# The chunk inverse of a delta-rule mixer: the masked factor as one 128x128 block with zero quadrants

## The reference, cut to what matters

```python
def wkv7_scan(s0, r, w, k, v, a, b):
    def step(s, inp):
        r_t, w_t, k_t, v_t, a_t, b_t = inp
        sa = jnp.einsum('bhij,bhj->bhi', s, a_t)
        s = s * w_t[:, :, None, :] + sa[..., :, None] * b_t[..., None, :] + v_t[..., :, None] * k_t[..., None, :]
        y = jnp.einsum('bhij,bhj->bhi', s, r_t)
        return s, y
    ...
    s_last, ys = lax.scan(step, s0, xs)
```

## Time and profile before

| | |
|---|---|
| median of 3 runs | 1065.11 us (1059.28 to 1065.58) |
| the profiled execution | 1064.27 us |
| its span, first to last instruction | 1062.5 us |
| granted TensorE clock, mean | 0.984 of full speed |
| busy in the span: PE / PEld / DVE / ACT / POOL | 985.0 / 728.9 / 552.9 / 374.0 / 461.4 us |

### The profile page before, as it was taken

How to read it: one execution, slowest core, us unless ns; L and a number is a source line. 1 busy time by engine, 2 the same in 40 slices (tenths; PEclk the granted TensorE clock), 3 DMA queues, 4 the chain that set the end, 5 groups by cost and what they waited for, 6 DMA issues and landing times. The chain is left out here.

```text
span 1062.5 us, 22807 instructions
## 1 busy us (share of the span) xinstructions
PE 985.0 (93%) x9433; PEld 728.9 (69%) x9433; DVE 552.9 (52%) x1176; ACT 374.0 (35%) x764; POOL 461.4 (43%) x505
## 2 busy tenths in 40 slices
PE   5999999979989989999999999999998999997885
PEld 4777787768878778888787888884554555554442
DVE  6587776757666527777455465333374222221125
ACT  3444446546666524444344440100121111111013
POOL 7647565257868457877732344410001222221110
PEclk9999999989999999999999999999998999999997
DMA  8022221030000056420351224408888999999985
GB/s 270 0 85 80 85 85 40 0 87 5 4 4 5 4 139 183 141 64 2 106 159 42 78 79 159 159 0 312 365 323 339 414 415 415 415 416 415 411 342 236
DMA packets 86000, 182.86 MB, mean 172 GB/s; under 512 B 9897, under 2 KB 59589, under 8 KB 78218
## 3 DMA queue, kind: packets, MB, share of 16 engines
q1 hardware_dynamic: 79325, 168.59, 43.7%
q0 software_dynamic: 5088, 8.43, 2.1%
q10 hardware_dynamic: 1485, 4.39, 1.1%
HBM read 172.98 MB, written 17.55 MB: 179 GB/s over the span
## 5 line engine op out<-in xcount | busy, mean ns | idle before, releaser
L2429 POOL DMA_INDIRECT d_y<-tl_xn,ex_sidx x32 | 32.1, 1002 | 113.2 <-DVE tl_xn L3021 105.6
L2424 POOL DMA_INDIRECT tl_xn<-d_tok,ex_gidx x16 | 16.9, 1053 | 139.4 <-DVEq L3012 76.5
L3017 DVE SCALAR_TENSOR_TENSOR ex_sg<-tl_psA,ex_slot_rs,ex_sg 128x128 f32<-128x128 f32 x32 | 11.2, 351 | 124.6 <-ACT ex_sg L2788 124.5
L264 PE MATMUL psv<-xT,w_sum 128*128 128x260 f32 x256 | 61.7, 384 | 1.2 <-DVE uv_gu L1702 0.6
L226 POOL TENSOR_TENSOR w_sum<-w 128x512 f32<-128x512 f32 x16 | 21.2, 1327 | 94.2 <-PE mg_w L264 94.0
L2788 ACT ACTIVATE ex_sg<-tl_psA,ex_slot_rs 128x128 f32<-128x128 f32 x32 | 11.8, 368 | 123.4 <-PE tl_psA L2622 122.1
L264 PEld LDWEIGHTS psv<-xT,w_sum 128*128 128x128 f32 x256 | 48.3, 190 | 9.9 <-issue 1.3
L264 PE MATMUL rk_ps<-xT,rk_w 128*128 128x260 f32 x208 | 50.1, 384 | 0.0
L264 PE MATMUL rk_ps<-xS,rk_w 128*128 128x260 f32 x200 | 48.6, 386 | 0.0
L264 PEld LDWEIGHTS rk_ps<-xT,rk_w 128*128 128x128 f32 x208 | 39.3, 190 | 6.7 <-issue 0.8
L264 PEld LDWEIGHTS rk_ps<-xS,rk_w 128*128 128x128 f32 x200 | 37.4, 190 | 8.0 <-issue 2.5
(11 more groups left out here) (637 smaller groups left out, 2713.6 us busy)
## 6 DMA issues: line engine op xcount, KB each, us to landing
wd<-in_moe_w_down SPq DMA_DIRECT2D x13, 1024.0 KB, 22.9
rk_w<-in_w_in SPq DMA_DIRECT2D x12, 1024.0 KB, 5.4
w_uv<-in_w_in SPq DMA_DIRECT2D x16, 512.0 KB, 5.3
w<-in_w_in SPq DMA_DIRECT2D x8, 1024.0 KB, 5.9
tl_x<-in_moe_w_down SPq DMA_DIRECT2D x8, 1024.0 KB, 19.0
xT<-in_moe_w_gate SPq DMA_DIRECT2D x5, 1024.0 KB
xT<-in_moe_w_up SPq DMA_DIRECT2D x5, 1024.0 KB
w<-in_proj_a SPq DMA_DIRECT2D x4, 1024.0 KB, 5.7
```

The source lines that it names most:

```text
L264: ins = eng.matmul(bank[:, 0:TH], w[:, k, :], x[:, k, :], start=(first and k == 0), stop=(last and k == NK // 2 - 1), skip_group_check=True)
L2424: eng.indirect_dma_start(out=xg[:, p % 2, :], out_offset=None, in_=m.d_tok, in_offset=bass.IndirectOffsetOnAxis(ap=gidx[:, p:p + 1], axis= ...
L2429: eng.indirect_dma_start(out=m.d_y2, out_offset=bass.IndirectOffsetOnAxis(ap=rows, axis=0), in_=yo[:, x, :], in_offset=None, bounds_check= ...
L3017: eng.scalar_tensor_tensor(out=sg[:, out, :], in0=psg[out][:, P:2 * P], scalar=scale, in1=sg[:, out, :], op0=ALU.mult, op1=ALU.mult).then_ ...
```

## The change

The change has two parts.

First, `rows_at` returns `own` always: in all chunks the heads stay in their halves, and R, X and `corrected` of every head use the quadrants (lo, lo) and (hi, hi) alone, unless the second part replaces them.

Second, from the second chunk on (`FIRST_WIDE = 1`), in all five levels (`WIDE_LEVELS = 5`), the masked V of a pair is a 128x128 block whose off-diagonal quadrants are zero. `masked_r` writes it in one VectorE operation for a group, 128x512 elements, reading R's result twice (a broadcast) against a mask that has zeros off the diagonal. X is then one product for each pair with a 128x128 stationary operand: 4 products in place of 8. R stays 8 products of 64x64 for a group and reads V out of the diagonal quadrants. The wide V lies in the dead columns of `m.br` and `m.k`, and the masks in those of `m.kk`; GpSimd builds the masks once in chunk 0 (`wide_masks`: a memset of 128x640, two copies of 64x320), between its last rows for chunk 1 and `with_diagonal`. R's results now lie 256 columns apart in PSUM, so that VectorE can read a group's with one stride.

```diff
+        VB = [m.br[:, :, 0:P], m.k[:, :, 0:P]]
+        FIRST_WIDE, WIDE_LEVELS, WIDE_OPS = 1, 5, 3
...
         def rows_at(t, lv, own, other):
-            return other if t and lv % 2 else own
+            return own

         def out_r(g, t, n):
-            return RB[g][:, t, n * CH:(n + 1) * CH]
+            return RB[g][:, t, n * 4 * CH:n * 4 * CH + CH]
...
+        def wide(c, lv):
+            return c >= FIRST_WIDE and lv < WIDE_LEVELS
+
+        def wide_mask(lv):
+            return m.kk[:, lv, 0:P].rearrange("p (h c) -> p h c", h=2).unsqueeze(1).to_broadcast([P, GP, 2, CH])
...
                 V = Vs[(lv + 1) % 2]
+                W = VB[(lv + 1) % 2]
                 if lv < NL - 1:
                     for t, n, p, own, other in heads(g):
                         at, to = rows_at(t, lv, own, other), rows_at(t, lv + 1, own, other)
-                        last = eng.matmul(out_r(g, t, n)[to], XQ[at, p, 1, :], V[at, p, :], start=True, stop=True)
+                        v = V[at, p, :] if not wide(c, lv) else W[at, p, wide_at(t, at)]
+                        last = eng.matmul(out_r(g, t, n)[to], XQ[at, p, 1, :], v, start=True, stop=True)
                     last.then_inc(s_w[g], 1)
...
+                if wide(c, lv):
+                    for t in range(2):
+                        for n in range(HP):
+                            p = g * GP + t * HP + n
+                            if lv < NL - 2:
+                                last = eng.matmul(out_xq(g, t, n), W[:, p, :], XQ[:, p, :, :], start=True, stop=True)
+                            else:
+                                last = eng.matmul(out_xq(g, t, n)[:, 0:CH], W[:, p, :], XQ[:, p, 0, :], start=True, stop=True)
+                    last.then_inc(s_x[g], 1)
+                    return
...
-                if lv == 0:
+                if wide(c, lv):
+                    if c == FIRST_WIDE and lv == 0:
+                        eng.wait_ge(s_bk, 4 * FIRST_WIDE)
+                        eng.wait_ge(s_wide, WIDE_OPS)
+                    r = b64(RB[g][:, 0]) if lv == 0 else RB[g][:, :, :].rearrange("p t (n c) -> p (t n) c", c=4 * CH)[:, :, 0:CH]
+                    eng.tensor_tensor(VB[(lv + 1) % 2][:, grp(g), :].rearrange("p n (h c) -> p n h c", h=2),
+                                      r.unsqueeze(2).to_broadcast([P, GP, 2, CH]),
+                                      wide_mask(lv), ALU.mult).then_inc(s_w_e[g], 1)
+                elif lv == 0:
...
+            def wide_masks():
+                eng.memset(m.kk[:, 0:WIDE_LEVELS, 0:P], 0.0).then_inc(s_wide, 1)
+                eng.wait_ge(s_wide, 1)
+                for rows in (lo, hi):
+                    eng.tensor_copy(m.kk[rows, 0:WIDE_LEVELS, rows], m.levels[rows, 1:1 + WIDE_LEVELS, :]).then_inc(s_wide, 1)
+                eng.wait_ge(s_wide, WIDE_OPS)
...
                 for g in range(G):
                     eng.wait_ge(s_ar[g], 4 * c + 4)
+                if c == 0:
+                    wide_masks()
                 for g in range(G):
                     with_diagonal(c + 1, g)
```

More of the change, by code:

```diff
@@ L928, in phase_chunks @@
             (sem("k_" + n) for n in ("step", "zero", "px", "pi", "bk", "fin", "sto", "out"))
-        s_lw, s_sv, s_sh, s_sv_e, s_sh_e, s_t2 = (sem("k_" + n) for n in ("lw", "sv", "sh", "sv_e", "sh_e", "t2"))
+        s_lw, s_sv, s_sh, s_sv_e, s_sh_e, s_t2, s_wide = (sem("k_" + n) for n in ("lw", "sv", "sh", "sv_e", "sh_e", "t2", "wide"))
         first_v, first_u = m.w_uv[:, 0, 0], m.w_uv[:, 0, 1]
@@ L985, in running, with wide_at @@
             return m.cum[:, :, c * (CH + 1) + first:c * (CH + 1) + last]
+        def wide(c, lv):
+            return c >= FIRST_WIDE and lv < WIDE_LEVELS
+        def wide_mask(lv):
+            return m.kk[:, lv, 0:P].rearrange("p (h c) -> p h c", h=2).unsqueeze(1).to_broadcast([P, GP, 2, CH])
+        def wide_at(t, rows):
+            return rows
         def a_rows(eng, c, g, rows, which):
@@ L1309, in masked_r @@
                 else:
-                    eng.tensor_tensor(by_type(V[:, grp(g), :]), two(RB[g], CH),
+                    eng.tensor_tensor(by_type(V[:, grp(g), :]), two(RB[g], 4 * CH, slice(0, CH)),
                                       m.levels[:, lv + 1, :].unsqueeze(1).unsqueeze(1).to_broadcast([P, 2, HP, CH]),
```

## The result

The changed kernel takes 1121.44 us (median of 4 runs, 1119.05 to 1122.69) against 1063.18 us for the kernel before (4 runs): a ratio of 1.0562 with a 95% interval of 1.0529 to 1.0595. The prediction was 1121, range 1104 to 1131. The profiled execution after took 1122.7 us with a span of 1121.0, 58.5 longer than before.

The account below looks back on a forecast made before the run. PE's queue was taken to bound the levels, with no slack in the phase behind. Seven chunks at 7.44 us more (52.1) plus 4.5 for chunk 0 gave 56.6 on 1064.3: 1121 us, range 1104 to 1131.

Parts of the forecast that it names:

- R in two quadrants: R's 8 products in the levels: 0.61 us from start to next step, against 0.28 in four quadrants, 0.33 more.
- X with 128 columns: Full-array X in levels 0 to 2: 1.03 us a step, in place of 0.46 to 0.55.
- X with 64 columns: Full-array X in levels 3 and 4: 1.0 us before R, 0.90 before X (0.95 in level 3's sum).
- The levels: The five levels of chunks 1 to 7 together: 6.86 us more a chunk.
- Masks: Each doubled mask 0.68 us instead of 0.41; one of ten a chunk on the path, 0.28 us (bounds 0.2, 0.6).
- corrected and chunk 0: The corrected products: 0.3 us more a chunk (bounds 0.1, 0.47); chunk 0: 4.5 us more (between 3.5 and 5.6).
- Wide masks on GpSimd: Building the wide masks once takes some 1.9 us, inside GpSimd's idle time, so it costs nothing.
- Shape changes that cost nothing: Rival: changing array shape between R and X is free, R 0.47 and X 0.88 us; 1106 us, chance 0.12.
- Masks longer than L1291: Rival: the doubled masks take 1.0 us each, reading PSUM twice through a broadcast; 1125 to 1131 us, chance 0.10.
- Every weight load exposed: Rival: each full-array record of X waits for its weight load, X 2.4 us instead of 1.03; 1217 us, chance 0.02.
- Records that cost alike wherever they stand: Rival: a step costs by its records, not columns or quadrants, so X gets shorter; 1053 us, chance 0.03.
- Levels paced by copies, within 1%: Rival: a mixture with the forecast where copies pace the levels and time stays within 1%; chance 0.03.

Follow-up runs that it names:

- the last experiment: The kernel before with the wide V and doubled masks (two operations per group and level), all products still 64x64 in four quadrants: 1071.48 us, ratio 1.0111.

## Why the prediction was right

It was right in time and in mechanism. That it hit the total to 1 us is luck: the levels were put too low by 4.5 us in seven chunks, and all other terms together too high by 3.6. The terms compare as follows.

**What bounds it.** Right. The levels were bound by PE's queue, the stretch behind had no slack (687.5 and 687.7 us to the end), and the longer chunks are the whole difference.

**R in two quadrants.** 0.61 predicted from L1057 to L1030, 0.61 measured. **X with 128 columns.** 1.03 predicted, 1.09 measured: the exit (0.20) and the steady records were right, the first record after a change of shape was mis-sized. It was taken from L1030, whose 4 records last 0.66; but X's 8 last 1.16 against L1533's 1.05, which is 0.11 and not 0.05. Six steps a chunk make 0.36 us of it. **X with 64 columns.** 1.0 and 0.95 predicted, 1.04 and 0.94 measured: L2517 with 36 columns was the right row.

**The levels.** 6.86 us a chunk more were predicted, on the 10.54 of chunk 4 (303.99 to 314.53); to 17.87 that is +7.33. Of the missing 0.47, 0.36 is X's first record, 0.05 is R of group 0 in level 0, which took 0.61 and not the 0.56 of the sum, and the rest lies in levels 3 and 4. Chunk 4 was the longest of before, too: the levels of the seven chunks add up to 72.6 us before and 125.1 after, so 52.5 us, 7.5 a chunk, where the sum had 48.0.

**Masks.** One of ten on the path, as said, and 0.68 us each. Its price was taken as 0.28 us a chunk, and the timelines with and without wide masks give 0.22. The far end of the range for this term did not occur, but the last experiment shows that it rested on the long steps. **corrected and chunk 0.** Chunk 0 takes 3.5 us more, from L1051 (now L1062) to the first R of chunk 1 (225.43 to 247.13 before, 226.30 to 251.51 after), where the sum had 4.5; R in one shape takes 0.47 there and not 0.51. What is left of the 57.5 is 1.5 us for masks and corrected in seven chunks, 0.2 a chunk, where the sum had 0.58. That is the mask alone: of the 0.3 taken for corrected next to nothing shows. Its records do take twice as long (the last of 32 starts 0.9 us behind the first, before 0.46), but the rest of the chunk hides it. These terms were over-sized by nearly as much as the levels were under-sized.

**Wide masks on GpSimd.** 1.9 us predicted, 1.64 measured (241.79 to 243.43), with 1.2 to spare. They started 3.7 us later than the prediction had them, behind another wait for VectorE (3.01), and still ended in time.

**The rivals.** Shape changes that cost nothing (1106): refuted, they cost 0.3 us there and back, 1.2 us a chunk in the kernel with X in column halves. Masks longer than L1291: refuted, 0.67 to 0.69. Every weight load exposed (1217): refuted, X's 8 records last 1.16 us. By the Trainium skill, TensorE: Matmul & The Clock Gate, Part 3, What overlaps and what doesn't, they would not overlap; the trace disagrees here as in the earlier trace rows. Records that cost alike wherever they stand (1053): refuted twice over: 8 full-array records take 1.09 us where 16 in four quadrants took 0.46 to 0.55, and R's 16 take 0.47 in two quadrants instead of 0.28. Levels paced by copies, within 1%: refuted, PE waits for no copy in them.

## What to carry to other kernels

Half as many instructions can be twice the time. Price each step by rows of the same shape elsewhere in the trace, and ask how many of its products can run side by side: here eight products of 64x64 took 0.28 us in four quadrants and 0.47 in two. Fewer columns need not help; on the full array X took 1.04 us with 64 and 1.09 with 128. Four independent 64x64 products in the four quadrants (row half and column half both alternating) are worth more than two 128x128 products with two zero quadrants each, and an exchange of halves that looks like a complication may be what fills them. An operation is hidden by something: before removing or moving it, or calling another one hidden, name the cover and ask what happens to it. And a total that hits can hide terms that miss: compare term by term, over all repetitions and not the one that was read.

## What the runs showed of the hardware that I had not expected

The first full-array record after a change of shape costs about 0.11 us beyond the steady step with non-transposing products of 128 columns (8 records in 1.16 us, against 1.05 where the shape holds), while L1030's transposes show 0.05 and so does X with 64 columns (8 records in 1.10). That this is a weight load and a stream that don't overlap is only argued. With a stationary block of 128 columns a float32 step hardly gets shorter with fewer moving columns: X takes 1.04 us with 64 and 1.09 with 128, all of the difference in the first record, while with 64 stationary columns it takes 0.61 and 1.03.
